# A diffusion step on one core: a block's result rows scattered by GpSimd with empty slots passed over, in place of two plain transfers

## The reference, cut to what matters

```python
D_MODEL, N_EXPERTS, TOP_K, D_FF = 1024, 32, 4, 1024
def routed_ffn(h, lp):                      # h: (384, 1024)
    logits = (h @ lp["w_router"] + lp["b_router"]).astype(jnp.float32)
    top_val, top_idx = lax.top_k(logits, TOP_K)
    gates = jax.nn.softmax(top_val, axis=-1)
...
    def run_block(args):                    # a block of rows of one expert e
        xb, e = args
        hb = xb @ w1[e] + b1[e]             # w1[e]: 1024 x 2048, 8 MB
        glu, lin = jnp.split(hb, 2, axis=-1)
        glu = jnp.minimum(glu, SWIGLU_LIMIT)
        lin = jnp.clip(lin, -SWIGLU_LIMIT, SWIGLU_LIMIT)
        act = glu * jax.nn.sigmoid(SWIGLU_ALPHA * glu) * (lin + 1.0)
        return act @ w2[e] + b2[e]          # w2[e]: 1024 x 1024, 4 MB
...
    return jnp.zeros_like(h).at[slot_t].add(ys * slot_g[:, None].astype(ys.dtype))
```

## Time and profile before

| | |
|---|---|
| median of 3 runs | 1799.97 us (1799.23 to 1815.21) |
| the profiled execution, its own time | 1797.29 us |
| its span, first to last instruction | 1795.4 us |
| PE busy | 1552.9 us (86%) |
| DVE busy | 841.4 us (47%) |
| bytes moved by DMA | 512.99 MB, 286 GB/s over the span |
| mean granted clock of PE | 0.916 |
| blocks of experts | 39; the first starts at 706.2 us, the last at 1728.2 us |

### The profile page before, as it was taken

The page is one execution under the profiler, slowest core; times in us unless marked ns, Lnnn a source line. Parts: engine busy times, 40 slices in busy tenths (PEclk is TensorE's granted clock), DMA queues, the critical chain, the costliest instruction groups (busy, mean ns, idle before and its releaser), DMA issues.

```text
span 1795.4 us, 29121 instructions
## 1 busy us (share of the span) xinstructions
PE 1552.9 (86%) x11145; PEld 754.9 (42%) x11146; DVE 841.4 (47%) x1211; ACT 260.2 (14%) x508; POOL 127.5 (7%) x193
## 2 busy tenths in 40 slices
PE   2699959598998996999998888899998889879994
PEld 0588825497895454333332222233222223222331
DVE  1433255767675545454433333444333344334445
ACT  0223313202211200111110100011010111101100
POOL 0000010100002100011100000011000000000111
PEclk8699968699998995999999899999998999999996
DMA  8524482300005472997799999979999999999996
GB/s 340 211 96 157 172 316 95 142 4 8 3 4 167 133 290 88 412 354 284 285 412 420 421 421 421 379 280 385 421 420 421 420 382 400 420 421 386 389 421 227
DMA packets 98525, 512.99 MB, mean 286 GB/s; under 512 B 14824, under 2 KB 17144, under 8 KB 45752
## 3 DMA queue, kind: packets, MB, share of 16 engines
q1 hardware_dynamic: 81928, 480.88, 66.6%
q10 hardware_dynamic: 11680, 18.49, 2.8%
q0 software_dynamic: 4848, 12.59, 2.0%
HBM read 493.12 MB, written 22.72 MB: 287 GB/s over the span
## 4 chain that ended last, share of the span: by engine, by line
PE 55%; DMA 21%; DVE 10%; SPq 6%; issue 4%; POOL 1%; ACT 1%; DVEq 0%; ACTq 0%; POOLq 0%
PE bank L689 52%; DMA work<-w_moe_in 17%; SPq L572 6%; PE bank L696 3%; DMA ring<-w_ada 1%; DVE work L1867 1%; DMA ring<-rows_d,dest 1%; DVE work L1598 1%; DVE work L1868 1%; DMA work<-mods_d 1%; DMA work<-b_moe_out 1%; DVE spare L1846 1%; DVE work L1607 0%; DVE work L1880 0%; DVE work L1691 0%
## 5 line engine op out<-in xcount | busy, mean ns | idle before, releaser
L689 PE MATMUL bank<-work 64*64 64x64 f32 (+3 forms) x5144 | 421.1, 306 | 46.6 <-DVE work L1846 43.3
L689 PE MATMUL bank<-ring,work 128*64 128x512 f32 (+1 forms) x1440 | 365.3, 600 | 13.3 <-ACT work L1175 7.0
L689 PEld LDWEIGHTS bank<-work 64*64 64x64 f32 (+2 forms) x5144 | 219.0, 139 | 233.4 <-issue 130.3
L689 PE MATMUL bank<-zbuf,work 128*64 128x512 f32 (+2 forms) x1560 | 265.8, 450 | 13.9 <-DVE zbuf L1846 13.6
L689 PEld LDWEIGHTS bank<-ring,work 128*64 128x64 f32 (+1 forms) x1440 | 123.7, 145 | 221.9 <-issue 204.5
L1175 ACT ACTIVATE work<-bank 128x512 f32<-128x512 f32 (+2 forms) x226 | 112.5, 514 | 622.0 <-PE bank L689 344.9
L689 PEld LDWEIGHTS bank<-zbuf,work 128*64 128x64 f32 (+2 forms) x1560 | 111.1, 142 | 158.4 <-issue 107.3
L689 PE MATMUL bank<-parts 128*128 128x512 f32 (+1 forms) x720 | 157.9, 382 | 3.4 <-DVE parts L423 3.4
L696 PE MATMUL bank<-ident,work 128*128 128x128 f32 (+2 forms) x404 | 82.5, 322 | 72.6 <-DVE work L1444 21.6
L689 PEld LDWEIGHTS bank<-parts 128*128 128x128 f32 x720 | 131.5, 191 | 29.9 <-issue 3.4
L1861 DVE TENSOR_SCALAR work<-bank 128x512 f32<-128x512 f32 x39 | 27.0, 691 | 236.3 <-PE bank L689 236.3
(11 more groups left out here) (228 smaller groups left out, 1054.6 us busy)
## 6 DMA issues: line engine op xcount, KB each, us to landing
work<-w_moe_in SPq DMA_DIRECT2D x192, 1024.0 KB, 24.0
ring<-w_moe_out SPq DMA_DIRECT2D x128, 1024.0 KB, 22.8
ring<-w_moe_in SPq DMA_DIRECT2D x64, 1024.0 KB, 18.5
ring<-w_ada SPq DMA_DIRECT2D x12, 2048.0 KB, 8.5
ring<-w_in SPq DMA_DIRECT2D x9, 2048.0 KB, 8.0
rows_d<-work ACTq DMA_DIRECT2D x76, 128.0 KB, 7.0
rows_d<-ky SPq DMA_DIRECT2D x11, 512.0 KB, 15.0
ring<-w_out SPq DMA_DIRECT2D x2, 2048.0 KB, 12.5
```

Of the source, the lines that this page charges most:

```text
L689: return pe.matmul(out, l, r, start=start, stop=stop)
```

## The change

The two plain transfers on ACT go. In their place POOL copies a column of a table `rows` to `row`, and scatters the 128 half rows of `ysb` by these indices; an empty slot has an index beyond the bound and is passed over. POOL then waits until the scatter has landed before it goes on. ACT's next copy to `ysb` waits for POOL's mark of that (`gpn`). As rows of empty slots are no longer written, SP fills the whole region `rows_d` with zeros, not only its upper part. DVE makes the table once, from the lists of input rows.

```diff
@@ SP
-                    for r in range(NE * HB, NBMAX * HB, P):
+                    for r in range(0, NBMAX * HB, P):
                         n = min(P, NBMAX * HB - r)
                         sp.dma_start(rows_d[r:r + n, :], at(ky, 0, D, rows=n)).then_inc(S["zfill"], 16)
...
-            for dst, src in ((crank, a["c_rank"]), (iota, a["c_iota"]), (ctok, a["c_tok"]),
+            for dst, src in ((crank, a["c_rank"]), (iota, a["c_iota"]), (ctok, a["c_tok"]), (crow, a["c_row"]),
@@ POOL
             def gather_listed(it):
                 gp.wait_ge(S["idxc"], 2)
                 gp.wait_ge(S["xgd"], 16 * it + 16)
-                gp.wait_ge(S["gpn"], 3 * it + 3)
+                gp.wait_ge(S["gpn"], 7 * it + 3)
...
+            def scatter_rows(it):
+                gp.wait_ge(S["yc"], it + 2)
+                gp.wait_ge(S["gpn"], 7 * it + 6)
+                gp.tensor_tensor(half[:, 12:13], half[:, 13:14], half[:, 13:14], ALU.mult).then_inc(S["gpn"], 1)
+                gp.tensor_copy(row[:, 0:1], rows[:, bass.ds(it, 1)]).then_inc(S["gpn"], 1)
+                gp.wait_ge(S["gpn"], 7 * it + 8)
+                gp.tensor_tensor(half[:, 14:15], half[:, 13:14], half[:, 13:14], ALU.mult).then_inc(S["gpn"], 1)
+                gp.indirect_dma_start(rows_d.rearrange("t (h n) -> (t h) n", h=2), bass.IndirectOffsetOnAxis(ap=row[:, 0:1], axis=0),
+                                      ysb, None, bounds_check=2 * NBMAX * HB - 1, oob_is_err=False).then_inc(S["yo"], 16)
+                gp.wait_ge(S["yo"], 16 * it + 16)
+                gp.tensor_tensor(half[:, 15:16], half[:, 13:14], half[:, 13:14], ALU.mult).then_inc(S["gpn"], 1)
...
             def block_of(it, last):
                 if not last:
                     gp.wait_ge(S["xtm"], it + 1)
                     gather_listed(it)
+                    scatter_rows(it)
...
-            gp.wait_ge(S["yo"], 32 * last_it + 32)
-            gp.wait_ge(S["gpn"], 3 * last_it + 3)
+            gp.wait_ge(S["yo"], 16 * last_it)
+            gp.wait_ge(S["gpn"], 7 * last_it + 3)
@@ ACT
                 sc.wait_ge(S["mult"], WC * it + (WC + ZQ_ALL))
-                sc.wait_ge(S["yo"], 32 * it + 32)
+                sc.wait_ge(S["gpn"], 7 * it + 3)
                 cp(ysb, B[2]).then_inc(S["yc"], 1)
-                sc.wait_ge(S["yc"], it + 2)
-                for h in range(2):
-                    dst = rows_q[bass.ds(it, 1), :, h * CH:(h + 1) * CH].rearrange("o t n -> t (o n)")
-                    sc.dma_start(dst, ysb[h * HB:(h + 1) * HB, :]).then_inc(S["yo"], 16)
@@ DVE
-            ve.wait_ge(S["zfill"], 16 * -(-NEXTRA * HB // P))
+            ve.wait_ge(S["zfill"], 16 * -(-NBMAX * HB // P))
...
-            ve.wait_ge(S["idxm"], 2)
+            ve.wait_ge(S["idxc"], 3)
+            L(ts(vacant, lists[:, :], 2.0 * NT * P, float(2 * NBMAX * HB), ALU.is_ge, M))
+            tt(rows[:, :], vacant, crow, A_).then_inc(S["routeq"], 1)
```

More of the change, by code:

```diff
@@ L133, in constants @@
     out["c_tok"] = (2 * (np.arange(P)[:, None] + P * np.arange(NT)[None]) - NOROW).astype(np.float32)
+    out["c_row"] = (2 * (s % HB) + s // HB + P * np.arange(NBMAX)[None, :]).astype(np.float32)
     out["c_iota"] = np.broadcast_to(np.arange(P, dtype=np.float32), (P, P)).copy()
@@ L182, in build @@
         lists = sb("lists", [P, NBMAX], U32)
+        rows = sb("rows", [P, NBMAX], U32)
+        row = sb("row", [P, 1], U32)
         dest = sb("dest", [P, NT * TOPK], U32)
@@ L285, in build @@
         brow = zf[:, 7720:7752]
+        vacant = zf[:, 8000:8000 + NBMAX]
+        crow = zf[:, 7944:7944 + NBMAX]
         selm = zf[:, 7752:7848].rearrange("p (j e) -> p j e", j=NT)
@@ L439, in build @@
         ]
-        NCONS2, NCONS3, NCONS4 = len(cons2), 2, 5
+        NCONS2, NCONS3, NCONS4 = len(cons2), 2, 6
         block = ctx.enter_context(nc.Block())
@@ L652, in gather_listed @@
                 gp.wait_ge(S["xgd"], 16 * it + 16)
-                gp.wait_ge(S["gpn"], 3 * it + 3)
+                gp.wait_ge(S["gpn"], 7 * it + 3)
                 gp.tensor_tensor(half[:, 12:13], half[:, 13:14], half[:, 13:14], ALU.mult).then_inc(S["gpn"], 1)
                 gp.tensor_copy(slots[:, 0:1], lists[:, bass.ds(it + 1, 1)]).then_inc(S["gpn"], 1)
-                gp.wait_ge(S["gpn"], 3 * it + 5)
+                gp.wait_ge(S["gpn"], 7 * it + 5)
                 gp.tensor_tensor(half[:, 14:15], half[:, 13:14], half[:, 13:14], ALU.mult).then_inc(S["gpn"], 1)
                 gather_rows()
+            def scatter_rows(it):
[9 more added lines that the diff above has]
+                gp.tensor_tensor(half[:, 15:16], half[:, 13:14], half[:, 13:14], ALU.mult).then_inc(S["gpn"], 1)
             gather_first()
-            gp.wait_ge(S["routeq"], 8)
+            gp.wait_ge(S["routeq"], 9)
             last_it = gp.value_load(tab[0:1, LAST:LAST + 1], min_val=NE - 1, max_val=NBMAX - 1)
@@ L1176, in _ @@
             sc.sem_inc(S["yc"], 1)
-            sc.sem_inc(S["yo"], 32)
             sc.wait_ge(S["condq"], 2)
@@ L1360, in _ @@
             last_it = sc.value_load(tab[0:1, LAST:LAST + 1], min_val=NE - 1, max_val=NBMAX - 1)
-            rows_q = rows_d.rearrange("(q t) n -> q t n", t=HB)
             def block_of(it, last):
```

## The result

The changed kernel takes 1836.78 us (median of 4 runs, 1830.88 to 1848.21), beside 1799.6 us for the kernel before (4 runs, 1795.46 to 1815.21). The ratio is 1.0198, 95% interval 1.012 to 1.0277. A second measurement gave 1835.88 against 1802.63 us, ratio 1.0221 (1.017 to 1.0272). Medians are of all executions, while ratios and their intervals use only those within 1.5% of the fastest of their kernel, so a ratio can differ by some tenths of a per cent from the quotient of the medians. The forecast was 1841 us, in a range from 1806 to 1895.

A forecast was written before the change was run, and what follows sets the result against it. Loop bound by weight loads in 30.93 us blocks, by PE in 23.47 us ones; 39 - 5.5 + 6.9 + 0.5 = +41 on 1797.3 gives 1838, 1841 us on the median, range 1806 to 1895.

The forecast's parts named there:

- Term 1: Expert loop: gather waits behind the scatter's landing, PE waits 3.3 us, with clock 4.3 us in nine blocks, +39 us.
- critical blocks: PE-paced 23.47 us blocks where DMA engines have gaps: 12 counted, nine losing 4.3 us, three with idle DMA nothing.
- in nine they are busy all along: Of 12 blocks in stretches with DMA gaps, nine keep DMA engines busy throughout, so gathers land in 6.9 us.
- hidden by the lead: PE-paced blocks with full DMA engines: 27.8 us stays under an expert's 30.9 us load, so no cost, for 3 us.
- Hidden in slow blocks: Weight-paced 30.93 us blocks: rows wanted at about +21.7 us, come at +17.6, hidden by 4 us.
- none in slow ones: Sign in the new profile: PE idles for the gather about 3.3 us in 23.47 us blocks, none in 30.93 us ones.
- The third rival: Expert loop: path 3 us longer makes POOL bound every block, +140, 1940 us; growth from 28.9 us a block; chance 0.15.
- Term 2: Expert loop: 3.67 MB fewer written by skipping empty slots, -5.5 us, bounds 0 and -8.7.
- Term 3: Attention: 16 more zero fills delay the w_ada load to 270.4 us, PE waits 6.9 us, no second wait; bounds 3 and 10.
- term 4: Loop start: DVE's table and constant, two 0.15 us instructions and a later wait ahead of its first copy, +0.5 us.
- The two rules: Skill's claims: DVE copies block GpSimd descriptors (+5 us a block); GpSimd transfers take 2.6 us here (term 1 nothing).
- the rival that rests on it: Expert loop: scatter and gather land in 4 us each, rows come at +11.7 before +14.27; 1802 us, chance 0.2.

The follow-up runs named there:

- run 2: Kernel before, plain transfers and few fills kept, plus POOL waiting for their landing before its next gather: 1824.1 us, ratio 1.012.
- run 3: Changed kernel, POOL issues the scatter, then the next gather, and only then waits for the scatter's landing: 1809.65 us, ratio 0.9995.
- run 4: Changed kernel, scatter of block b-1 put behind the gather for block b+1, POOL still waiting for the landing: 1807.2 us, ratio 0.999.
- run 9: Changed kernel plus two small POOL instructions between the scatter's landing and the next gather: 1953.56 us (2 executions), ratio 1.0843.
- run 7: Changed kernel, scatter of block b-1 behind the gather for block b+1, and 28 fills moved behind the load of w_out: 1815.64 us, ratio 1.0117.
- run 8: Changed kernel, scatter behind the following gather, 28 fills behind the load of w_out, empty slots written too: 1814.01 us, ratio 1.0087.
- run 10: Changed kernel, scatter behind the following gather, 28 fills spread over the input projection's weight loads: 1799.68 us beside 1805.97, ratio 0.9982.
- run 11: Changed kernel in its own order, with only the 28 fills spread over the input projection's weight loads: 1829.69 us, ratio 1.0161.

## Why the prediction was right

*Term 1, the gather behind the scatter.* Step by step for a fast block, forecast and block 8 of the changed kernel: scatter starts +2.05, +2.20; landed +9.05, +8.89 (POOL goes on at +8.97); gather starts +10.65, +10.59; landed +17.55, +17.34; PE waits 3.3, 3.05 us; clock 1.0, and PE is busy 24.32 us in place of 23.12, so 1.2 us. A block took 27.42 us where 27 to 28 stood in the forecast. Taking the landing from the plain write at the same place (7.0 us) was the choice that counted: the scatter's median is 7.2. Its reason, that the write took this "whether the DMA engines were full or not", doesn't hold: every plain write of the kernel before flew while the DMA engines were busy for 0.93 or more of the time, also in blocks with gaps. The gaps come later in the block: in block 2 of the changed kernel the share is 0.96 from 778.8 to 786.6 us and 0.35 from 786.6 to 799.9. Over all blocks the gather starts somewhat later than in block 8, at +11.3 in the median. Runs 2, 3 and 4 show that the wait ahead of the gather is the cause.

*How many blocks, and how much in each.* Here a term of the sum was mis-sized, by 16 us. In the critical blocks I wrote 4.3 us nine times, 39 us. Measured: blocks 1, 3, 5 and 7 lost 5.8, 1.7, 3.3 and 1.4 us against 23.48, blocks 17 and 19 8.5 us together, blocks 28 and 35 1.7 and 0.2 us: 22.6 us. Four blocks (2, 4, 6, 18) were quiet, not three, and in blocks 3, 7, 28 and 35 the gather landed in 3.3 to 4.5 us and not in 6.9. The step that failed is "in nine they are busy all along": a window's mean rate doesn't say what a gather meets 11 us into the block. Against that, blocks 29 to 34 lost 3.3 us by the traces, where I had "hidden by the lead", and blocks 36 and 37 lost 8.2 us, of which the last block gave back 7.5: before, PE stood in it for its weights and their copies, and after the delay these had come. Three rows of the kernel before show it, with 1.81, 1.42 and 4.09 us of idle time; the changed kernel has none of these waits.

```profile
1738.47 1.08 PE L689 MATMUL bank<-work 128*64 128x512 f32 x4 [1.81 <-DVE work L1846]
1740.97 1.78 PE L689 MATMUL bank<-spare,work 128*64 128x512 f32 x4 [1.42 <-DVE spare L1846]
...
1760.01 3.68 PE L689 MATMUL bank<-ring,work 128*64 128x512 f32 x8 [4.09 <-DMA ring<-w_moe_out]
```

I had not looked at the end of the loop; that it came out nearly even is luck.

*Hidden in slow blocks.* That these blocks cost nothing was right, but the sign "none in slow ones" was not. Blocks 15, 16 and 27 wait for nothing, 14 and 26 for 0.2 and 0.4 us. But blocks 10 to 13, 22 to 25 and 31 to 33, also among those that were over 28 us before, wait too, for 2.1 to 5.4 us each. Blocks 8 to 16 as a whole are no longer for it (261.7 us against 263.6), since the loads set their pace: in most of the blocks that wait PE is ready for the rows at +14.3, on a lead that the delay makes last longer. Blocks 32 and 33 waited 5.4 and 5.1 us and still took 30.9 and 30.6 us, the slow kind's length.

*The third rival.* It did not come about, because the path was as forecast, but its mechanism is real: run 9, with most blocks of 31 to 33 us, gave 1953.6 us where the rival had 1940 for 30.9 us. Its threshold of 28.9 us stays untested, since no run lies between.

*Term 2, the bytes.* 3.9 MB less, forecast 3.67. Worth -5.5 us by the forecast; blocks 8 to 16 became 1.9 us shorter in spite of the waits, blocks 20 to 27 0.1. By the loops that are free of PE's waits it is 4 to 8 us (runs 7 and 8). The size is right to a few microseconds, and the trace of the changed kernel alone can't show it better.

*Term 3, the zeros.* The chain of waits and PE's row in the changed kernel:

```profile
252.18 18.98 DMA ring<-w_ada
...
271.21 1.88 PE L707 MATMUL bank<-ring,condT 128*2 128x512 f32 x8 [6.54 <-DMA ring<-w_ada]
```

Landed at 271.17 us, forecast 270.4; the wait 6.54 us, forecast 6.9; no second wait. The rest of the 12.7 us by which the loop starts later isn't the change's as far as these runs go: run 2, with no fill more than before, starts its loop at 717.8 us, and programs that are identical up to there differ by 12 us (runs 7 and 8) and by 32 (runs 10 and 11). In single executions this also hides whether term 4 (0.5 us) is right.

In all: forecast +41; by the traces 6.5 for the zeros and 25.0 for the loop with its end, 31.5 us, and by the medians of the two measurements 37 and 33 us. The sign and its cause were right. Critical blocks were counted too dear by 16 us. That the forecast still came out only 4 us high is in part luck: the saving of bytes showed less than 5.5 us, blocks 29 to 37 cost 4 us net of what the end gave back, and the time ahead of the loop was some 6 us longer than the change explains.

*The two rules.* The scatter takes POOL 1.03 to 2.00 us to issue (median 1.04) and the gather 1.07 to 2.20, with DVE's copies all around. The Trainium skill, SBUF — State Buffer, section "SBUF: two separate sides", gives some 3100 ns in place of some 620 for a transfer issued by GpSimd, as a whole, when it falls together with a DVE copy, 2.5 us more. The trace shows at most 1.1 us more of issuing, and in the landing little: the plain writes issued by ACT landed in a median of 7.0 us, the scatter in 7.2. Gathers landed in 2.4 to 3.1 us in the four quiet blocks and in 6.6 to 7.2 us in blocks 8 to 15. The Trainium skill, DMA: Bandwidth & Descriptors, section "Anatomy of one DMA — SWDGE (gpsimd) path", has a fit that gives 2.6 us for 256 KB, an estimate from that page. The trace agrees with it only where the DMA engines have gaps, and there the rival that rests on it came true (block 2 of 23.48 us). It is the first in the list of rivals, and the prediction calls it the second.

## What to carry to other kernels

A wait for a transfer's landing costs what stands behind it in that engine's program, not the transfer: put such a wait behind the next issue that others need, and the same scatter costs nothing that can be measured. Work out the slack in one block, then count for which blocks it holds; past the length at which the other resource gives no more cover, each microsecond counts in nearly every block (37 us of time for each here). A bulk fill that nobody waits for still delays what is behind it on the DMA engines, so put it where the rate is low and nothing is due.

## What the runs showed of the hardware

- The granted clock in attention isn't the same from one execution to the next. With the same program ahead of the loop it was 0.50 from 235 to 340 us in run 10, and 0.67 and 0.74 in run 11, and the loop started at 735.2 and 703.1 us; in runs 7 and 8 it was 0.50 and 0.66 from 235 to 300 us, and the loop started at 728.3 and 716.2 us. Most of the scatter of the kernel before's times (1792.32 to 1827.96 us in 31 runs) may be this; what decides it stays open.
- With 28 fills queued (27 of 512 KB, one of 256), packets of the instruction queue came some 2 and 5 us later than without them (373.8 for 372.0 us, 380.8 for 375.9), and PE stood for 4.3 us in two pauses (4.7 and 4.1 us in runs 7 and 8).
- An indirect scatter of up to 128 half rows lands in 6.0 to 8.3 us, like a plain write of all 128 (5.8 to 8.3 us). In block 18 the scatter took 6.1 us while the DMA engines were busy for 0.83 of the time and moved 346 GB/s; the gather behind it took 2.8 us at 0.10 and 24 GB/s, its own bytes included. The longest scatter, 8.3 us in block 19, had them busy all along (1.00, 401 GB/s). No scatter of the changed kernel met DMA engines that were busy for less than 0.82 of its flight, so whether the direction or the load makes the difference from the gathers wasn't tried.
